# Two heads in one turn: the one-map heads of a hybrid attention taken in pairs on one Trainium2 core

## What is computed

```python
# A: two maps, values of width 128
s = einsum('bqhmd,bkhmd->bhmqk', qb, k) * scale
s = where(dist >= 0, s + bias[None, :, None], NEG)
p = softmax(s, axis=-1)
attn = p[:, :, 0] - lam * p[:, :, 1]
o = einsum('bhqk,bkhd->bqhd', attn, v)
...
# B and C: one map, values of width 64; which keys count is part of the mask
s = where(mask, einsum('bqhd,bkhd->bhqk', q, k) * scale + bias, NEG)
o = einsum('bhqk,bkhd->bqhd', softmax(s, axis=-1), v)
```

## Time and profile before

| | us |
|---|---|
| median of 3 runs | 3533.17 |
| lowest and highest | 3527.28, 3534.81 |
| the profiled execution, its own time | 3531.7 |
| its span, first to last instruction | 3529.9 |

### The profile page before, as it was taken

How to read it: one execution, slowest core, us unless ns; L and a number is a source line. 1 busy time by engine, 2 the same in 40 slices (tenths; PEclk the granted TensorE clock), 3 DMA queues, 4 the chain that set the end, 5 groups by cost and what they waited for, 6 DMA issues and landing times. The chain is left out here.

```text
span 3529.9 us, 49263 instructions
## 1 busy us (share of the span) xinstructions
PE 3370.2 (95%) x21362; PEld 2761.5 (78%) x21362; DVE 1903.7 (54%) x2685; ACT 1202.2 (34%) x1692; POOL 8.3 (0%) x8
## 2 busy tenths in 40 slices
PE   7999999799999999999997889999999999999998
PEld 5888877778788888888876878788887757878886
DVE  4434665645454445434675664443456766457475
ACT  3323343134332233223443143332233274344243
POOL 0000000000000000000000000000000000000000
PEclk9999998889999999999998899999999999999999
DMA  3323223013123232323221024132223203323232
GB/s 122 106 91 105 79 79 93 3 56 131 61 97 101 95 102 90 105 92 105 80 74 36 3 78 131 62 101 95 96 96 119 84 1 102 114 72 102 89 100 73
DMA packets 78198, 301.70 MB, mean 85 GB/s; under 512 B 8946, under 2 KB 9586, under 8 KB 77344
## 3 DMA queue, kind: packets, MB, share of 16 engines
q1 hardware_dynamic: 77984, 298.56, 25.8%
HBM read 296.40 MB, written 6.06 MB: 86 GB/s over the span
## 5 line engine op out<-in xcount | busy, mean ns | idle before, releaser
L323 DVE TENSOR_TENSOR w_lo<-ring,w_hi 128x1024 fp32r<-128x1024 f32 (+1 forms) x508 | 652.5, 1286 | 507.5 <-ACT w_hi L316 507.1
L341 PE MATMUL ps<-xa_hi,w_hi 128*128 128x512 f32 x1728 | 688.3, 398 | 16.5 <-DVE w_lo L323 12.6
L343 PE MATMUL ps<-xa_hi,w_lo 128*128 128x512 f32 x1728 | 677.2, 392 | 0.0
L342 PE MATMUL ps<-xa_lo,w_hi 128*128 128x512 f32 x1728 | 677.2, 392 | 0.0
L316 ACT ACTIVATE w_hi<-ring 128x1024 fp32r<-128x1024 f32 (+1 forms) x508 | 555.1, 1099 | 343.9 <-DMA ring<-in_ffn_in_dram 73.6
L341 PE MATMUL ps<-xb_hi,w_hi 128*128 128x512 f32 x1248 | 489.4, 392 | 0.0
L343 PE MATMUL ps<-xb_hi,w_lo 128*128 128x512 f32 x1248 | 485.8, 389 | 0.0
L342 PE MATMUL ps<-xb_lo,w_hi 128*128 128x512 f32 x1248 | 485.6, 389 | 0.0
L341 PEld LDWEIGHTS ps<-xa_hi,w_hi 128*128 128x128 f32 x1728 | 327.3, 189 | 100.1 <-DVE w_lo L323 14.1
L342 PEld LDWEIGHTS ps<-xa_lo,w_hi 128*128 128x128 f32 x1728 | 327.4, 189 | 69.3 <-issue 2.9
L343 PEld LDWEIGHTS ps<-xa_hi,w_lo 128*128 128x128 f32 x1728 | 327.0, 189 | 69.3
(11 more groups left out here) (359 smaller groups left out, 3488.0 us busy)
## 6 DMA issues: line engine op xcount, KB each, us to landing
ring<-in_ffn_in_dram SPq DMA_DIRECT2D x176, 512.0 KB, 3.4
ring<-in_ffn_out_dram SPq DMA_DIRECT2D x64, 704.0 KB, 4.1
ring<-in_mix_in_dram SPq DMA_DIRECT2D x58, 512.0 KB, 3.4
ring<-in_up_dram SPq DMA_DIRECT2D x44, 512.0 KB, 3.4
ring<-in_w_in_dram SPq DMA_DIRECT2D x22, 512.0 KB, 3.4
ring<-in_down_dram SPq DMA_DIRECT2D x16, 704.0 KB, 4.1
ring<-in_mix_out_dram SPq DMA_DIRECT2D x16, 512.0 KB, 4.1
ring<-in_xk_dram SPq DMA_DIRECT2D x16, 512.0 KB, 3.5
```

Of the source, the lines that this page charges most:

```text
L323: dve.tensor_tensor(core.w_lo[j][:, 0:width], core.ring[j][:, 0:width], core.w_hi[j][:, 0:width].bitcast(F32), ALU.subtract).then_inc(self ...
L341: pe.matmul(out, hi, x_hi, start=(opens and k == tiles[0]), stop=False)
L342: pe.matmul(out, hi, x_lo, start=False, stop=False)
L343: last = pe.matmul(out, lo, x_hi, start=False, stop=(closes and k == tiles[-1]))
```

## The change

The list `units` holds the A heads as before, but of the B and C heads only every second one: a unit with `h >= A_HEADS` now stands for the heads h and h + 1, which lie on the two halves of the same tiles. There are 32 units, of which 16 are pairs (`apart`). Scores, bias pass and exponentials of a pair take the form that an A unit has: two maps on two halves of rows, in two banks. The mask of a C pair is added to both maps in one instruction of twice the width. The two maps of a pair are then multiplied and transposed each for itself, in two turns, which use the banks 4 and 5 one after the other; `n_turns` counts them. The gather alternates between the two heads, whose outputs are the two halves of the partitions of one bank, and the store takes both in one instruction.

```diff
-    units = [(h, i) for h in range(HEADS) for i in range(QT)]
+    units = [(h, i) for h in (*range(A_HEADS), *range(A_HEADS, HEADS, 2)) for i in range(QT)]
+    apart = [h >= A_HEADS for h, _ in units]
+    n_turns = np.cumsum([0] + [1 + two for two in apart]).tolist()
...
             def scores(n):
...
-                    pe.wait_ge(topped, n_maps[n - 1])
-                for q, k, w in maps(h):
+                    pe.wait_ge(topped, 2 * (n - 1))
+                for w in range(2):
                     pe.matmul(ps[:, 2 * (n % 2) + w, 0:(i + 1) * P], big[half(w), q, i * P:(i + 1) * P],
                               big[half(w), k, 0:(i + 1) * P], start=True, stop=True).then_inc(scored, 1)
 
             def turn(n):
                 h, i = units[n]
-                pe.wait_ge(shared, n + 1)
-                if n >= 2:
-                    pe.wait_ge(turned_out, n - 1)
-                for k in range(i + 1):
-                    last = pe.transpose(ps[:, 4 + n % 2, k * P:(k + 1) * P], probs[:, n % 4, 0, k * P:(k + 1) * P],
-                                        core.c("ident"))
-                last.then_inc(turned, 1)
+                for t in range(n_turns[n], n_turns[n + 1]):
+                    pe.wait_ge(shared, t + 1)
+                    if t >= 2:
+                        pe.wait_ge(turned_out, t - 1)
+                    for k in range(i + 1):
+                        last = pe.transpose(ps[:, 4 + t % 2, k * P:(k + 1) * P],
+                                            probs[:, n % 4, t - n_turns[n], k * P:(k + 1) * P], core.c("ident"))
+                    last.then_inc(turned, 1)
...
                 for k in range(i + 1):
-                    last = pe.matmul(to, v_n[:, k, at:at + (P if h < 4 else C)], turned_sb[:, n % 4, k * P:(k + 1) * P],
-                                     start=(k == 0), stop=(k == i))
+                    cols = slice(k * P, (k + 1) * P)
+                    if apart[n]:
+                        for w in range(2):
+                            at = (2 * A_HEADS + h + w - 4) * C
+                            last = pe.matmul(ps[half(w), bank, 0:P], v_n[:, k, at:at + C], turned_sb[:, (t + w) % 4, cols],
+                                             start=(k == 0), stop=(k == i))
...
+                    if h >= 8 and i:
+                        dve.wait_ge(scored, 2 * (n + 1))
+                        dve.tensor_tensor(kept, s, unpicked[:, i - 1, 0:width].unsqueeze(1).to_broadcast([P, 2, width]),
+                                          ALU.add).then_inc(picked, 1)
...
+                    if apart[done]:
+                        for w, p in enumerate((first, second)):
+                            dve.tensor_scalar(p, p, stats[:, done % 4, w, 2:3], None, ALU.mult).then_inc(shared, 1)
...
             def store(n):
...
+                to = h if h < 4 else 4 + (h - 4) // 2
+                act.activation(out[:, to, i * P:(i + 1) * P], ps[:, 6 + n % 2, 0:P], ACT.Copy).then_inc(stored, 1)
...
-                act.wait_ge(turned, n + 1)
-                act.activation(turned_sb[:, n % 4, 0:(i + 1) * P], ps[:, 4 + n % 2, 0:(i + 1) * P],
-                               ACT.Copy).then_inc(turned_out, 1)
+                for t in range(n_turns[n], n_turns[n + 1]):
+                    act.wait_ge(turned, t + 1)
+                    act.activation(turned_sb[:, t % 4, 0:(i + 1) * P], ps[:, 4 + t % 2, 0:(i + 1) * P],
+                                   ACT.Copy).then_inc(turned_out, 1)
```

More of the change, by code:

```diff
@@ L2509, in block2_attention, with tiles @@
     out = core.y
-    units = [(h, i) for h in range(HEADS) for i in range(QT)]
-    def maps(h):
+    units = [(h, i) for h in (*range(A_HEADS), *range(A_HEADS, HEADS, 2)) for i in range(QT)]
+    apart = [h >= A_HEADS for h, _ in units]
+    n_turns = np.cumsum([0] + [1 + two for two in apart]).tolist()
+    def tiles(h):
         if h < 4:
-            return [(AQ + h, AK + h, w) for w in range(2)]
+            return AQ + h, AK + h
         n = h % 4
         q, k = (BQ, BK) if h < 8 else (CQ, CK)
-        return [(q + n // 2, k + n // 2, n % 2)]
-    n_maps = np.cumsum([0] + [len(maps(h)) for h, _ in units]).tolist()
+        return q + n // 2, k + n // 2
     with stage(nc, "scored", "topped", "exped", "inverted", "shared", "turned", "turned_out", "gathered",
@@ L2529, in scores @@
                 h, i = units[n]
+                q, k = tiles(h)
                 if n >= 2:
[L2532 to L2533 removed]
+                    pe.wait_ge(topped, 2 * (n - 1))
+                for w in range(2):
                     pe.matmul(ps[:, 2 * (n % 2) + w, 0:(i + 1) * P], big[half(w), q, i * P:(i + 1) * P],
@@ L2538, in turn @@
                 h, i = units[n]
-                pe.wait_ge(shared, n + 1)
-                if n >= 2:
-                    pe.wait_ge(turned_out, n - 1)
-                for k in range(i + 1):
-                    last = pe.transpose(ps[:, 4 + n % 2, k * P:(k + 1) * P], probs[:, n % 4, 0, k * P:(k + 1) * P],
-                                        core.c("ident"))
-                last.then_inc(turned, 1)
+                for t in range(n_turns[n], n_turns[n + 1]):
[6 more added lines that the diff above has]
+                    last.then_inc(turned, 1)
             def gather(n):
                 h, i = units[n]
-                pe.wait_ge(turned_out, n + 1)
+                pe.wait_ge(turned_out, n_turns[n + 1])
                 if n >= 2:
                     pe.wait_ge(stored, n - 1)
-                at = h * P if h < 4 else (2 * A_HEADS + h - 4) * C
-                to = ps[:, 6 + n % 2, 0:P] if h < 4 else ps[half(h % 2), 6 + n % 2, 0:P]
+                bank, t = 6 + n % 2, n_turns[n]
                 for k in range(i + 1):
-                    last = pe.matmul(to, v_n[:, k, at:at + (P if h < 4 else C)], turned_sb[:, n % 4, k * P:(k + 1) * P],
-                                     start=(k == 0), stop=(k == i))
+                    cols = slice(k * P, (k + 1) * P)
[4 more added lines that the diff above has]
+                                             start=(k == 0), stop=(k == i))
+                    else:
+                        last = pe.matmul(ps[:, bank, 0:P], v_n[:, k, h * P:(h + 1) * P], turned_sb[:, t % 4, cols],
+                                         start=(k == 0), stop=(k == i))
                 last.then_inc(gathered, 1)
@@ L2573, in turn_of @@
                 if done is not None:
[L2574 to L2577, removed]
+                    dve.wait_ge(exped, 2 * (done + 1))
+                    dve.reciprocal(stats[:, done % 4, :, 2:3], stats[:, done % 4, :, 1:2]).then_inc(inverted, 1)
+                    first, second = (probs[:, done % 4, w, 0:(units[done][1] + 1) * P] for w in range(2))
                 if new:
@@ L2581, in turn_of @@
                     if n >= 4:
[L2583 to L2595, removed]
+                        dve.wait_ge(turned, n_turns[n - 3])
@@ new lines, in turn_of @@
+                    s = ps[:, 2 * (n % 2):2 * (n % 2) + 2, 0:width]
+                    kept = probs[:, n % 4, :, 0:width]
+                    if h >= 8 and i:
+                        dve.wait_ge(scored, 2 * (n + 1))
+                        dve.tensor_tensor(kept, s, unpicked[:, i - 1, 0:width].unsqueeze(1).to_broadcast([P, 2, width]),
+                                          ALU.add).then_inc(picked, 1)
+                        picked_now[0] += 1
+                        dve.wait_ge(picked, picked_now[0])
+                        s = kept
@@ L2596, in turn_of @@
+                    for w in range(2):
+                        dve.wait_ge(scored, 2 * n + w + 1)
+                        dve.tensor_tensor_reduce(kept[:, w], s[:, w], bias[:, h + w if apart[n] else h, (QT - 1 - i) * P:S],
+                                                 -C ** -0.5, 3e38, ALU.add, ALU.min,
+                                                 stats[:, n % 4, w, 0:1]).then_inc(topped, 1)
                 if done is not None:
                     dve.wait_ge(inverted, done + 1)
-                    if k == 2:
+                    if apart[done]:
+                        for w, p in enumerate((first, second)):
+                            dve.tensor_scalar(p, p, stats[:, done % 4, w, 2:3], None, ALU.mult).then_inc(shared, 1)
+                    else:
@@ L2599, in turn_of @@
                         dve.tensor_scalar(stats[:, done % 4, 1, 2:3], stats[:, done % 4, 1, 2:3], core.lam,
                                           None, ALU.mult).then_inc(weighted, 1)
[L2601 to L2606, removed]
+                        dve.tensor_scalar(first, first, stats[:, done % 4, 0, 2:3], None, ALU.mult).then_inc(weighted, 1)
@@ L2608, in _ @@
+                        dve.wait_ge(weighted, 2 * (done + 1))
+                        dve.scalar_tensor_tensor(first, second, stats[:, done % 4, 1, 2:3], first, ALU.mult,
+                                                 ALU.add).then_inc(shared, 1)
             picked_now = [0]
@@ L2612, in _ @@
```

(6 more changed lines are left out.)

## The result

| | before | changed |
|---|---|---|
| median, us | 3530.82 (4 runs) | 3510.03 (4 runs) |
| lowest and highest | 3527.28, 3534.81 | 3503.96, 3512.69 |
| the profiled execution, its own time | 3531.7 | 3512.69 |
| its span | 3529.9 | 3510.9 |
| ratio to before, 95% interval | | 0.9948 (0.9932 to 0.9963) |

The changed kernel is faster by 0.5%, 20.8 us between the medians; forecast were 22.8 us and 3510.4.

The account below looks back on a forecast made before the run. TensorE, busy for 95% of the span, was taken to bound the kernel. Pairing B heads (2 x 6.2 us) and C heads (2 x 5.2 us) saves 22.8 us, giving a median of 3510.4 us, range 3504 to 3520.

Parts of the forecast that it names:

- What bounds the stage: Attention stage: B and C heads are held by TensorE, and a B head uses it at half of what it holds.
- Scores of a pair: B and C pairs: one head's scores in place of two, 512-wide scores at 1.12 to 1.13 us with four records.
- Gathers of a pair: B and C pairs: no more than one head's gather; 16 alternating 512-wide records take 0.92 us, about what eight take.
- The rival's 11.2 us a pair: Gathers that don't overlap: 2.6 us more a pair, B and C pairs 11.2 us, total 3518.0 us; chance 0.10.
- Turns: B and C pairs: all transposes stay, adding 1.2 us a pair (1.1 to 2.0), so TensorE's sum is 8.6 us.
- C pairs at 10.0 us, bound by VectorE: C pairs: VectorE bounds at 10.0 us (9.6 to 10.4) against 15.24 for two heads; 5.2 us less, twice.
- ScalarE just below TensorE: B pairs: ScalarE's load computed at 9.0 and under 8.95 us a pair, taken as just below TensorE's 8.6.
- this one: Rival that ScalarE sets the pace: a pair takes some 10.5 us, 18.0 us less in all, 3515.2 us; chance 0.14.
- The clock: Rival that TensorE's clock falls to 1.2 GHz in the pairs: 16.1 us a pair, 4.4 us slower, 3537.6; chance 0.04.
- The sum: Whole stage: B pairs 2 x 6.2 plus C pairs 2 x 5.2, 22.8 us less, median 3510.4 us; chance 0.70.
- 3.2 us less: Behind the stage: 3.2 us go if the clock there does not run low, part of the range's lower end, 3504.

Follow-up runs that it names:

- b_pairs_only: The changed kernel with only the B heads in pairs and the C heads each for itself as before; median 3517.0 us, ratio 0.9965.
- scores_in_turn: The changed kernel with the second head's scores of each pair issued behind the turn; median 3532.6 us, ratio 1.0014; run again, one execution, 3537.04 us.
- no_mask: The changed kernel without adding the mask of keys not picked in C pairs, so the index's choice is left out; median 3502.27 us, ratio 0.9928.
- shares first: The changed kernel with VectorE doing unit n's shares before unit n + 2's mask and bias pass; median 3502.87 us, ratio 0.9927; again (shares_first_2) 3501.26, 0.9931.
- two_stores: The changed kernel with each pair's store done as two instructions of 64 partitions; median 3509.44 us, ratio 0.9946.
- gathers_in_turn: The changed kernel with each pair's gather doing head h over all blocks, then head h + 1, not alternating; median 3511.41 us, ratio 0.9949.

## Why the prediction was right

*What bounds the stage.* Right. B heads were held by TensorE with half of its rows and columns idle; the pairs that fill them are still held by TensorE (17.25 of 17.40 us busy), and b_pairs_only shows their share alone.

*Scores of a pair at the price of one head.* Right: 1.13 us for four records, and scores_in_turn shows that it is their being neighbours that does it.

*Gathers of a pair at no more than one head's.* Right: 1.02 us, as eight records took. The neighbour row, `spread_to_heads`, was a sound bound though its weights and accumulation differ. It gave 0.92 us for 16 records. The rival's 11.2 us a pair was measured at 11.07 and 11.16 when both heads were put on one half, though the gathers were 2.2 of it and not 2.6. What I had not thought of is that heads gathered one after the other still overlap in part.

*Turns.* 1.2 us a pair taken, 8.6 in all; measured 8.73 and 8.70, so the turns cost 1.3. The second turn starts right behind the first.

*C pairs at 10.0 us, bound by VectorE.* 9.87 measured, and no_mask shows the bound. That it came so near is in part luck: VectorE's work was 9.1 us where 9.6 were computed, and 10.0 was a choice between 9.6 and 10.4. The 0.77 us of waits on top hang on VectorE's order: with shares first the pair takes 9.23, just over the work. The double-width mask costs what a line through the single widths gives: 0.69, 0.94 and 1.23 us.

*ScalarE just below TensorE.* Right in sign. Its load was less than computed (15.80 of 17.40 us are 7.9 a pair; computed were 9.0 and 8.95), and yet four more stores a pair were not absorbed everywhere (two_stores): as its trace reads, what counted was which copy TensorE waited for, and not ScalarE's sum. Of the rivals this one was nearest. On the Trainium skill's sentence on copies out of PSUM ("TensorEngine Tiling (Array Packing)", PSUM Bottleneck): the page says it of tiling that makes TensorE four times as fast, and here it is twice at most. The trace agrees that ScalarE comes next, at 15.80 of 17.40 us busy, and not that it bounds; the gain it would have left was 18.0 us, the stage's was 22.4.

*The clock.* Right for this kernel: 1.00 through all pairs. But the argument, that a share of 0.86 of busy time is as safe as the A part's 0.85, is not shown to be the reason: scores_in_turn fell to half clock with TensorE busy for 23.87 of 25.60 us, and stayed there. The chance of 0.04 was for a mechanism that is real one edit away.

*The sum.* 22.8 us against 22.4 in the stage, of which B 11.7 where 12.4 were forecast, and C 10.7 where it was 10.4 (b_pairs_only); the two misses partly cancel. In the total, 19.0 between the two profiled executions, 20.8 between the first medians, and 0.5% by both ratios. That the median of 3510.03 lies 0.4 from the forecast 3510.4 is luck: single times spread by nine us, and the part behind the stage moved as well. The prediction had allowed it 3.2 us less; in the profiled executions it took 3.6 more. Two stretches of it differ in the granted clock, first in the changed kernel:

```profile
2899.59:2919.59 20.00, 20.00 (x100) 17.71 (x101) 10.37 (x16) 10.31 (x15) 0.00 (x0) 0.76 0.19 79
3077.59:3099.59 22.00, 21.17 (x79) 14.36 (x78) 6.18 (x9) 6.05 (x10) 0.00 (x0) 0.94 0.09 29
```

and at the same distances behind the stage before:

```profile
2922.15:2942.15 20.00, 20.00 (x106) 17.47 (x107) 11.05 (x16) 11.70 (x17) 0.00 (x0) 0.83 0.20 80
3100.15:3122.15 22.00, 21.17 (x89) 15.68 (x88) 7.59 (x10) 7.30 (x12) 0.00 (x0) 1.00 0.16 48
```

Counted by the same matmuls, the changed kernel falls 1.4 us behind in the first stretch and 1.7 in the second, which is 3.1 of the 3.6; the rest lies behind the last matmul. Over the traces of kernels that are alike from there on, that part took 605.9 (two_stores) to 611.6 us (shares_first_2), and 607.8 in gathers_in_turn, which is what the kernel before had. Both traces of the changed kernel had 611.3 and 611.4, and there is one trace of the kernel before; so that these 3.6 us are chance, and no cost of the change, is likely but not shown.

## What to carry to other kernels

When the engine that bounds a stage works on half of its rows or columns, put the work for the other half directly beside it: neighbours on different halves of rows (scores) or columns (gathers) ran at the price of one here. With one step between them the second scores cost their full time, 2.8 us a pair; the clock fell besides, and both together took the whole gain. Then sum up the other engines for the new period before counting the gain: here VectorE came up with the mask in C, and ScalarE within a tenth of the pair. And read a gain of half a per cent in the stage's own period, which repeats to hundredths of a us, and not in times that vary by nine.

## What the runs showed of the hardware that was not expected

**Overlap of column halves has a reach.** Sixteen gather records on two column halves take 1.02 us alternating, 1.07 in runs of four, 1.51 in runs of eight, and 1.89 when both are on one half. In the unit of width 384, runs of six take 1.07 us against 0.80 alternating and 1.45 on one half, in that of width 256, runs of four 0.60 against 0.59 and 1.02. So one change of halves saves some 0.4 us each time (1.89 - 1.51, 1.45 - 1.07, 1.02 - 0.60), and a record on one half costs 1.89 / 16 = 0.12: as an estimate, three to four records of the other half can run beside those ahead of them.

**TensorE at 1.2 GHz for some 85 us, with hardly a gap.** With the scores of the two row halves apart from each other, the granted clock fell in three of three traces and came back only when turns and gathers alone were left, in one of them after 84.6 us of which TensorE was busy for 84.13. The same matmuls as neighbours ran at 1.00 through all pairs in both traces of the changed kernel. Short waits (0.45 to 1.56 us) stood just ahead of each fall, but waits of 1.22 and 1.64 us in the changed kernel did nothing. Nor are separated scores needed for a fall: in both traces of shares first the clock fell in the drain, behind a wait of 1.93 us, and was back some 3 us later. What decides it is open.
